# Seven quarter products in place of eight in the gate and up products of one feed-forward, with its hidden tiles in two passes

## The chip, the cores and the metric

One core of one Trainium2 chip runs the whole program. The metric is the device time of one execution, in microseconds (us). TensorE (PE in the profile) multiplies, with its weight loads shown apart as PEld; VectorE (DVE), ScalarE (ACT) and GpSimd (POOL) do the elementwise work; SyncE (SP) issues the weight transfers.

## The reference, cut to what matters

Two layers (DEPTH = 2) work on 256 latent and 256 context tokens of width 1024. Each layer has a feed-forward, a token-mixing part with three branches, and a second feed-forward. All arrays are float32.

```python
D_MODEL, SEQ, CTX_LEN, DEPTH, FFN_HIDDEN = 1024, 256, 256, 2, 2816

def swiglu(h, w_gu, w_down):
    g, u = jnp.split(h @ w_gu, 2, axis=-1)
    return (jax.nn.silu(g) * u) @ w_down

def ada_ffn_half(h, shift, scale, gate, norm_w, w_gu, w_down):
    return h + 0.5 * gate * swiglu(modulate(rms_norm(h, norm_w), shift, scale), w_gu, w_down)
```

The change is in the second layer's first `ada_ffn_half`. There `h` holds context and latent tokens together (512 columns), since the context is still read by the token mixing behind it. The second layer's second feed-forward works on the 256 latent tokens alone.

## The kernel before, in words

Activations lie feature by feature: 128 features in the partitions, tokens in the free dimension. `u` (the normed and modulated input) is 8 chunks of 128 features by 512 tokens. Weights come from HBM as a stream of panels of 128 x 2048 float32 (1 MB) in the order of use, into a ring of three (`RING`). A panel goes to the ring when the one three places before it has been left (`panel_left`, L899).

A float32 product is made of three matmuls on values rounded to a 32-bit format that TensorE reads faster (`fp32r`): hi x hi, lo x hi and hi x lo. For that, each half panel (128 x 1024, `HALF`) is rounded by ScalarE into `w_hi` (`round_half`, L972), and VectorE writes the rest, source minus rounded, into `w_lo` (`rest_of_half`, L2132). There are three places for halves (`HALVES`), so a half is rounded once the half three before it has been used (`half_used`). `split_matmul` (L1519) issues the three matmuls of one 128-deep step. Activations are split the same way: `u_hi`/`u_lo`, `hidden_hi`/`hidden_lo`.

A feed-forward (`ffn`) makes 22 hidden tiles (`FC`) of 128 features. A tile takes a gate product and an up product, each of 8 steps of three matmuls over all tokens (`std`), each in one PSUM bank; banks 0 to 3 are used in turn (`number[key] % 4`, `free_bank`). Tiles go in pairs: two gates, two ups. ScalarE takes the gate out of its bank with Silu (L1032), VectorE multiplies with the up bank (L2267), ScalarE rounds into `hidden_hi` (L1025), VectorE writes `hidden_lo` (L2273). When all 22 tiles are there, 8 down products (22 steps each) are made, and VectorE adds each, times the gate of the modulation, to `h` (`residual`, L2232).

Ahead of the feed-forward stands the norm (`norm`), in two parts of 256 tokens. VectorE scales a chunk into one of four slots of `sq` (L2172), ScalarE adds the shift and rounds into `u_hi` (L1004), VectorE writes `u_lo` (L2180); TensorE runs the first two gate tiles chunk by chunk behind it (`normed`, `streamed`).

Each engine's work is in program order, written by hand: the class `Splits` says between which other steps ScalarE and VectorE round the next halves. GpSimd has work only in the attention and delta parts (L920, L939, L949, L957); during the feed-forwards it has none.

In the last layer's later stages the 256-token activations are placed 48 elements further (`NARROW`), against weights that start at multiples of 64 elements.

Of the kernel before, what the change touches and what calls it, by code (L numbers as in the profile page):

```python
# [31 lines left out]
P = 128  # L32
# [37 lines left out]


# [68 lines left out]
def stream(inp):  # L140
# [150 lines left out]

def panel_kinds():
# [45 lines left out]


KINDS, START, ADA_AT = panel_kinds()  # L340
SPLITS = [n for n, k in enumerate(KINDS) if k == "split"]
N_PANELS = len(KINDS)


def product_owners():
# [52 lines left out]
    return number, owner, counts  # L398


def backbone(nc, wts, par_d, cst_d, mod_d, x_d, c_d, out_d):
    number, owner, counts = product_owners()

    split_before = np.cumsum([0] + [k == "split" for k in KINDS]).tolist()
    with ExitStack() as ctx:
# [3 lines left out]
        def sem(name):  # L409
# [41 lines left out]
        y_whole = [at("ya", 36, 4), at("yb", 40, 4), at("yc", 44, 4)]  # L451
        m_whole_hi = at("m_hi", 0, DC, F32R)
# [131 lines left out]

        def heads(ap):
# [24 lines left out]
        ab_read = sem("ab_read")  # L610
# [24 lines left out]
        gmv_root_ready = sem("gmv_root_ready")  # L635
# [37 lines left out]
        outs_rooted = sem("outs_rooted")  # L673
        outs_inverted = sem("outs_inverted")
# [3 lines left out]
        softplus_log = sem("softplus_log")  # L678
        decays_ready = sem("decays_ready")
# [3 lines left out]
        gamma_summed = sem("gamma_summed")  # L683
        gamma_read = sem("gamma_read")
# [2056 lines left out]
```

## Time and profile before

| | |
|---|---|
| median of 3 runs | 2488.67 us (2485.3 to 2489.74) |
| profiled execution, its own time | 2488.27 us |
| its span | 2486.5 us |
| PE busy | 2388.7 us (96%) |
| DVE busy | 1451.9 us (58%) |
| ACT busy | 942.5 us (38%) |
| POOL busy | 133.3 us (5%) |
| HBM read | 306 MB, 124 GB/s over the span |
| share of PE in the chain that ended last | 90% |

The profile gives times from the span's start. "PEclk" is the clock granted to TensorE, 1.00 being 2.4 GHz and 0.50 being 1.2 GHz. Matmul ends are modelled, so the spacing of starts tells more than the length of one. The gate and up products that the change touches begin at about 1462 us; those behind the first two gate tiles run from 1479.8 us.

### The profile page before, as it was taken

Reading aid. Unit: us, or ns where it says so; the run is one execution under the profiler, and the core shown is the slowest. Engines: PE = TensorE matmul, PEld = TensorE weight load, DVE = VectorE, ACT = ScalarE, POOL = GpSimd, SP = SyncE. Lnnn points to the kernel's source line nnn. Section 1 sums busy time; section 2 is a strip of 40 time slices with the busy share of each in tenths; the row PEclk is TensorE's granted clock in tenths of the full one; section 3 lists DMA queues with packets and bytes.
Section 4 is the critical chain, followed back from the end, with each engine's and each line's share of the span. In section 5 each row is a group of like instructions: output and inputs, shape, how many; then the busy total and the mean of one; then the engine's idle time right before and its main releaser. Section 6 shows DMA issues by size and latency. Waiting matters only on the chain.

```text
span 2486.5 us, 37740 instructions
## 1 busy us (share of the span) xinstructions
PE 2388.7 (96%) x15782; PEld 2028.2 (82%) x15782; DVE 1451.9 (58%) x2257; ACT 942.5 (38%) x1537; POOL 133.3 (5%) x170
## 2 busy tenths in 40 slices
PE   5999999999989999999999999999999988999999
PEld 4888888857878888888888888888886778899999
DVE  5877666356567465587755553333454657566655
ACT  2322223356544422233232232232244654444543
POOL 0000000003033000000000000000000203200000
PEclk8999999999999999999999999999999999999999
DMA  7545443211200043335554432222322220044554
GB/s 279 216 174 201 170 156 114 102 35 69 74 30 2 35 169 113 130 127 197 195 187 170 161 115 89 102 102 96 108 102 85 85 85 2 19 170 171 182 190 170
DMA packets 44664, 309.66 MB, mean 125 GB/s; under 512 B 5072, under 2 KB 6224, under 8 KB 7632
## 3 DMA queue, kind: packets, MB, share of 16 engines
q1 hardware_dynamic: 44208, 305.98, 33.8%
q8 instruction: 126, 2.06, 0.3%
q10 hardware_dynamic: 288, 1.27, 0.1%
q14 instruction: 42, 0.34, 0.0%
HBM read 306.18 MB, written 1.05 MB: 124 GB/s over the span
## 4 chain that ended last, share of the span: by engine, by line
PE 90%; DVE 5%; ACT 3%; issue 2%; DMA 1%; SPq 0%; POOL 0%; ACTq 0%; DVEq 0%
PE bank L1519 75%; PE bank L1876 7%; PE bank L1512 2%; PE bank L1793 1%; PE bank L1816 1%; DVE u_lo L2180 1%; DVE w_lo L2132 1%; PE bank L1802 1%; DVE sq L2172 1%; PE bank L1550 1%; ACT w_hi L972 1%; PE bank L1734 1%; DMA mod_par<-in_mod 0%; PE bank L1562 0%; ACT work L1290 0%
## 5 line engine op out<-in xcount | busy, mean ns | idle before, releaser
L2132 DVE TENSOR_TENSOR w_lo<-ring,w_hi 128x1024 fp32r<-128x1024 f32 x420 | 510.4, 1223 | 670.5 <-ACT w_hi L972 666.0
L1519 PE MATMUL bank<-u_hi,w_hi 128*128 128x512 f32 (+1 forms) x2272 | 813.8, 358 | 26.8 <-DVE w_lo L2132 13.9
L1519 PE MATMUL bank<-u_hi,w_lo 128*128 128x512 f32 (+1 forms) x2272 | 803.0, 353 | 0.0
L1519 PE MATMUL bank<-u_lo,w_hi 128*128 128x512 f32 (+1 forms) x2272 | 802.7, 353 | 0.0
L972 ACT ACTIVATE w_hi<-ring 128x1024 fp32r<-128x1024 f32 x420 | 443.0, 1059 | 818.8 <-PE bank L1519 804.5
L1519 PEld LDWEIGHTS bank<-u_hi,w_hi 128*128 128x128 f32 x2272 | 430.9, 190 | 95.6 <-issue 22.0
L1519 PEld LDWEIGHTS bank<-u_lo,w_hi 128*128 128x128 f32 x2272 | 431.0, 190 | 59.8
L1519 PEld LDWEIGHTS bank<-u_hi,w_lo 128*128 128x128 f32 x2272 | 431.0, 190 | 57.7
L1519 PE MATMUL bank<-hidden_hi,w_hi 128*128 128x512 f32 (+1 forms) x722 | 257.9, 357 | 0.0
L1519 PE MATMUL bank<-hidden_hi,w_lo 128*128 128x512 f32 (+1 forms) x722 | 257.2, 356 | 0.0
L1519 PE MATMUL bank<-hidden_lo,w_hi 128*128 128x512 f32 (+1 forms) x722 | 257.2, 356 | 0.0
L1876 PE MATMUL bank<-work 64*64 64x64 f32 (+1 forms) x3472 | 193.6, 237 | 30.9 <-DVE work L2617 11.3
L1876 PEld LDWEIGHTS bank<-work 64*64 64x64 f32 (+1 forms) x3472 | 174.1, 149 | 47.0 <-issue 17.2
L1519 PEld LDWEIGHTS bank<-hidden_hi,w_hi 128*128 128x128 f32 x722 | 135.6, 188 | 21.4 <-issue 1.6
L1519 PEld LDWEIGHTS bank<-hidden_lo,w_hi 128*128 128x128 f32 x722 | 135.7, 188 | 20.0
L1519 PEld LDWEIGHTS bank<-hidden_hi,w_lo 128*128 128x128 f32 x722 | 135.7, 188 | 19.9
L920 POOL TENSOR_TENSOR work<-work,small 128x512 f32<-128x512 f32 (+1 forms) x48 | 42.8, 897 | 1696.7 <-DVE small L2481 1696.4
L2113 DVE SCALAR_TENSOR_TENSOR ada_sum<-ring,cond,ada_sum 128x1024 f32<-128x1024 f32 x98 | 125.4, 1279 | 0.6
L1025 ACT ACTIVATE hidden_hi<-sg 128x512 fp32r<-128x512 f32 (+1 forms) x88 | 49.9, 579 | 146.6 <-DVE sg L2267 146.6
L2267 DVE TENSOR_TENSOR sg<-sg,bank 128x512 f32<-128x512 f32 (+1 forms) x88 | 53.1, 616 | 64.2 <-PE bank L1519 64.2
L1032 ACT ACTIVATE sg<-bank 128x512 f32<-128x512 f32 (+1 forms) x88 | 46.7, 535 | 114.8 <-PE bank L1519 114.8
L2113 DVE SCALAR_TENSOR_TENSOR rt<-ring,cond,rt 128x1024 f32<-128x1024 f32 x70 | 89.4, 1278 | 0.0
(234 smaller groups left out, 2451.4 us busy)
## 6 DMA issues: line engine op xcount, KB each, us to landing
ring<-in_wts SPq DMA_DIRECT2D x288, 1024.0 KB, 4.8
h<-in_x SPq DMA_DIRECT2D x8, 256.0 KB, 4.4
par<-in_par ACTq DMA_DIRECT2D x2, 620.0 KB, 5.9
out<-h SPq DMA_DIRECT2D x8, 128.0 KB, 3.5
cst<-in_cst SPq DMA_DIRECT2D x1, 704.0 KB, 12.2
mod_par<-in_mod SPq DMA_DIRECT2D x1, 96.0 KB, 12.1
cond<-in_c SPq DMA_DIRECT2D x1, 8.0 KB, 1.8
```

Source lines behind the costliest of these rows:

```text
L920: pool.tensor_tensor(some, some, ri[:, a % 4:a % 4 + 1].to_broadcast([P, keys.stop]), ALU.mult).then_inc(att_scaled, 1)
L972: act.activation(w_hi[:, b % HALVES, :], half_source(n % RING, part), ACT.Copy).then_inc(weights_rounded, 1)
L1025: act.activation(h_hi[:, 2 * i + c, 0:w], sg[:, c, 0:w], ACT.Copy).then_inc(hidden_rounded, 1)
L1032: act.activation(sg[:, c, 0:w], bank[(q0 + c) % 4][:, 0:w], ACT.Silu).then_inc(drained["a"], 1)
L1512: last = weights.used(pe.matmul(out, lhsT, rhs, start=n == 0, stop=n == len(parts) - 1))
L1519: last = weights.used(pe.matmul(out, lhs[a], rhs[b], start=start and n == 0, stop=stop and n == 2))
L1550: last = pe.matmul(bank[7 - unit % 2][32 * j:32 * j + 32, 0:256], C("pick")[:, 32 * s:32 * s + 32], total[:, j, :], start=s == 0, stop=s = ...
L1734: last = pe.transpose(bank[4 + n % 2][0:QK, hd * P:(hd + 1) * P], tile[:, at:at + QK], ident)
L1876: return pe.matmul(out, lhsT, rhs, start=start, stop=stop)
L2113: last = stt(total, panel[:, kk, :, :], cond[:, k, s:s + 1], total, ALU.mult, ALU.add)
L2132: tt(w_lo[:, b % HALVES, :], half_source(n % RING, part), w_hi[:, b % HALVES, :].bitcast(F32), ALU.subtract).then_inc(panel_left[n % RING] ...
L2267: tt(sg[:, c, 0:w], sg[:, c, 0:w], bank[(q0 + 2 + c) % 4][:, 0:w], ALU.mult).then_inc(drained["v"], 1)
```

## The change

For hidden tiles 2 to 21 (`PLAIN = 2` stay as they were) of layer 1's first feed-forward, gate and up are computed together by Strassen's scheme in Winograd's form. The panel of a tile is cut into four quarters (128 x 512, four steps of 128): "11" and "12" the gate weights for features 0 to 511 and 512 to 1023, "21" and "22" the up weights for the same. The activations are cut into features 0 to 511 and 512 to 1023, tokens 0 to 255 (EARLY) and 256 to 511 (LATE). Of these come:

- four sums of weight quarters for each tile, s1 = 21 + 22, s2 = s1 - 11, s3 = 11 - 21, s4 = 12 - s2, made by GpSimd into the four slots of `sq`;
- four sums of the activations ("folds"), made once by GpSimd from `whole`, the unrounded `u`, and split in hi and lo by ScalarE and VectorE;
- seven products a tile, each 4 steps of three matmuls over 256 columns, in half a bank each, in the order p1, p6, p2, p5, p7, p3, p4;
- four additions by VectorE that put gate and up together from them, into `sum_work`, one operand from PSUM and one from SBUF in each, and one copy of p1 by ScalarE.

A tile now has seven quarter units to round and rest, in place of two halves. `w_hi`/`w_lo` are flat, with six places for quarters, which are put 16 elements further (`SHIFT`). The hidden tiles go in two passes, 0 to 11 and 12 to 21, each followed by its own 8 down products (12 steps, then 10) and additions to `h`, since `whole`, the folds and `sum_work` take arena space of the hidden tiles. Semaphores of other stages are merged to free numbers; they order the same steps.

```diff
+SUMMED = ((1, 0),)
+PASSES = ((0, 12), (12, FC))
+PLAIN = 2
+SHIFT = 16
+SUM_PRODUCTS = (("p1", "a"), ("p6", None), ("p2", "v"), ("p5", None), ("p7", "v"), ("p3", None), ("p4", "v"))
+QUARTERS = ("11", "s2", "12", "s1", "s3", "s4", "22")
```

GpSimd:

```diff
+            def sums_of(l, f):
+                tt = pool.tensor_tensor
+                for i in range(PLAIN, FC):
+                    n = START[l, "sum", f, i]
+                    before = 6 * (sum_before[n] - 1)
+                    a11, a12, a21, a22 = [quarter_of(n, at) for at in range(4)]
+                    s1, s2, s3, s4 = [sq[:, at, :] for at in range(4)]
+                    pool.wait_ge(panel_in[n % RING], 16 * (n // RING + 1))
+                    if i == PLAIN:
+                        pool.wait_ge(tokens_summed, PART_AT[l, 2 * f] + len(PARTS[l, 2 * f]))
+                        pool.wait_ge(tokens_spread, PART_AT[l, 2 * f] + len(PARTS[l, 2 * f]))
+                    if before >= 0:
+                        pool.wait_ge(quarter_rest_ready, before + 4)
+                    tt(s1, a21, a22, ALU.add).then_inc(sums_made, 1)
+                    pool.wait_ge(sums_made, sum_count(n, "s1"))
+                    tt(s2, s1, a11, ALU.subtract).then_inc(sums_made, 1)
+                    if before >= 0:
+                        pool.wait_ge(quarter_rest_ready, before + 5)
+                    tt(s3, a11, a21, ALU.subtract).then_inc(sums_made, 1)
+                    if before >= 0:
+                        pool.wait_ge(quarter_rest_ready, before + 6)
+                    pool.wait_ge(sums_made, sum_count(n, "s2"))
+                    tt(s4, a12, s2, ALU.subtract).then_inc(sums_made, 1)
+                    if i == PLAIN:
...
+                        pool.wait_ge(whole_ready, 2 * DC * (SUMMED.index((l, f)) + 1))
+                        tt(t1, up[:, :, LATE], up[:, :, EARLY], ALU.subtract).then_inc(sums_made, 1)
...
```

ScalarE, ahead of the tiles:

```diff
+            def summed_ffn(l, f):
+                for part, places in enumerate(PARTS[l, 2 * f]):
+                    for k in range(DC):
+                        act.wait_ge(u_rest_ready, DC * (PART_AT[l, 2 * f] + part) + k + 1)
+                        for c, cols in places:
+                            act.activation(whole[:, k, cols], whole[:, k, cols], ACT.Identity,
+                                           bias=mods[:, l, 6 * f * DC + k, c:c + 1]).then_inc(whole_ready, 1)
...
+                plain_gate(0)
+                plain_gate(1)
+                splits.freed(first + 2)
...
```

TensorE, one tile:

```diff
+                def panel(i):
+                    for what, _ in SUM_PRODUCTS:
+                        key = (l, what, f, i)
+                        w2 = weights.quarter()
+                        free_bank(key)
+                        for k in range(4):
+                            last = split_matmul(bank_of(key)[:, LATE if what in ("p6", "p5", "p3") else EARLY],
+                                                [x[:, k, :] for x in w2], [x[:, k, :] for x in operands[what]], k == 0, k == 3)
+                        last.then_inc(product_made, 1)
...
```

VectorE, one tile:

```diff
+                def panel(i, at):
...
+                    splits.freed(u0)
+                    splits.freed(u0 + 1)
+                    if i > max(at, PLAIN):
+                        made(i - 1)
+                    splits.freed(u0 + 2)
+                    wait_product(dve, p2)
+                    wait_drained(dve, p1)
+                    tt(sum_work[:, c11:U2 + 1:U2 - c11, :], two(p2),
+                       sum_work[:, P1:P1 + 1, :].to_broadcast([P, 2, SEQ]), ALU.add).then_inc(drained["v"], 1)
+                    splits.freed(u0 + 3)
+                    if i > max(at, PLAIN):
+                        rest(i - 1, at)
+                    splits.freed(u0 + 4)
+                    wait_product(dve, p7)
+                    wait_drained(dve, p2)
+                    step(tt(sum_work[:, U3:U3 + 2, :], two(p7), sum_work[:, U2:U2 + 1, :].to_broadcast([P, 2, SEQ]), ALU.add))
+                    step.wait()
+                    tt(sum_work[:, c22, :], sum_work[:, U3, :], bank_of(p7)[:, LATE], ALU.add).then_inc(drained["v"], 1)
+                    splits.freed(u0 + 5)
+                    splits.freed(u0 + 6)
+                    wait_product(dve, p4)
+                    tt(sum_work[:, c21:c21 + 4:3, :], two(p4), sum_work[:, U3:U3 + 2, :], ALU.add).then_inc(drained["v"], 1)
+                    wait_drained(dve, p4)
```

(`splits.freed(v)` rounds or rests all units whose place is free once unit v - 1 has been used; `u0` is the tile's first unit.)

VectorE before, in the gate and up tiles: a round of this block serves two tiles (four halves, two products, two hidden rests).

```order
L2132 TENSOR_TENSOR w_lo<-ring,w_hi 128x1024 [waits weights_rounded] x4
L2267 TENSOR_TENSOR sg<-sg,bank 128x512 [waits drained_by_act,product_made] x2
L2273 TENSOR_TENSOR hidden_lo<-sg,hidden_hi 128x512 [waits hidden_rounded] x2
```

VectorE of the change, one tile (`panel`, from `splits.freed(u0)` to the addition of p4; L2482 is the rest of a unit, L2625 gate times up, L2630 the hidden rest, L2649, L2657, L2659 and L2663 the additions):

```order
L2482 TENSOR_TENSOR w_lo<-sq,w_hi 128x512 [waits weights_rounded,drained_by_dve]
L2482 TENSOR_TENSOR w_lo<-ring,w_hi 128x512 [waits weights_rounded]
L2625 TENSOR_TENSOR sum_work<-sum_work 128x512 [waits gated]
L2482 TENSOR_TENSOR w_lo<-ring,w_hi 128x512 [waits weights_rounded]
L2649 TENSOR_TENSOR sum_work<-bank,sum_work 128x2x256 [waits drained_by_act,product_made]
L2482 TENSOR_TENSOR w_lo<-sq,w_hi 128x512 [waits weights_rounded]
L2630 TENSOR_TENSOR some_lo<-sum_work,some_hi 128x512 [waits hidden_rounded]
L2482 TENSOR_TENSOR w_lo<-ring,w_hi 128x512 [waits weights_rounded]
L2657 TENSOR_TENSOR sum_work<-bank,sum_work 128x512 [waits drained_by_dve,product_made]
L2659 TENSOR_TENSOR sum_work<-sum_work,bank 128x256 [waits dve_step]
L2482 TENSOR_TENSOR w_lo<-sq,w_hi 128x512 [waits weights_rounded] x2
L2663 TENSOR_TENSOR sum_work<-bank,sum_work 128x2x256 [waits product_made]
```

Four instructions a tile on VectorE became thirteen. GpSimd, which had nothing here, has four a tile (the change; the first row waits for the rest of the tile before, whose s1 it overwrites):

```order
L1094 TENSOR_TENSOR sq<-ring 128x512 [waits quarter_rest_ready,panel_in0,sums_made]
L1096 TENSOR_TENSOR sq<-sq,ring 128x512 [waits sums_made]
L1099 TENSOR_TENSOR sq<-ring 128x512 [waits quarter_rest_ready]
L1103 TENSOR_TENSOR sq<-ring,sq 128x512 [waits sums_made,quarter_rest_ready]
```

ScalarE where the norm ends and the tiles begin, before:

```order
L1004 ACTIVATE u_hi<-sq,mods 128x256 [waits chunk_scaled] x3
L972 ACTIVATE w_hi<-ring 128x1024 [waits half_used]
L1032 ACT_TABLE_LOAD
L1032 ACTIVATE sg<-bank 128x512 [waits product_made] x2
```

and of the change:

```order
L1212 ACTIVATE u_hi<-whole,mods 128x256 [waits chunk_scaled] x3
L1231 ACTIVATE whole<-whole,mods 128x256 [waits u_rest_ready] x16
L1237 ACT_TABLE_LOAD
L1237 ACTIVATE plain_sg<-bank 128x512 [waits product_made] x2
L1180 ACTIVATE w_hi<-ring 128x1024 [waits half_used]
```

The half that the second up tile needs is now rounded behind sixteen additions of the shift, a table load and two Silus.

## Rows read from the trace of the kernel before

**Rows 1.** The page: busy time, share of the span and instructions of each engine.
```profile
PE 2388.7 (96%) x15782; PEld 2028.2 (82%) x15782; DVE 1451.9 (58%) x2257; ACT 942.5 (38%) x1537; POOL 133.3 (5%) x170
```

**Rows 2.** Stretch, length; PE, PEld, DVE, ACT, POOL busy (count); PEclk, DMA share, GB/s.
```profile
1482.00:1707.00 225.00, 225.00 (x994) 186.34 (x993) 78.78 (x84) 68.39 (x86) 0.00 (x0) 1.00 0.28 99
```

**Rows 3.** Timeline of PE, 512 columns: first and last of 55 rows.
```profile
1499.70 0.39 PE L1519 MATMUL bank<-u_hi,w_hi 128*128 128x512 f32 x1
...
1511.94 0.39 PE L1519 MATMUL bank<-u_hi,w_hi 128*128 128x512 f32 x1
```

**Rows 4.** The same, 256 columns, 48 elements further: first and last of 55.
```profile
2249.84 0.28 PE L1519 MATMUL bank<-u_hi,w_hi 128*128 128x256 f32 x1
...
2255.96 0.28 PE L1519 MATMUL bank<-u_hi,w_hi 128*128 128x256 f32 x1
```

**Rows 5.** The same, 256 columns, not moved: first and last of 20.
```profile
1472.00 0.28 PE L1519 MATMUL bank<-u_hi,w_lo 128*128 128x256 f32 x1
...
1474.28 0.28 PE L1519 MATMUL bank<-u_lo,w_hi 128*128 128x256 f32 x1
```

**Rows 6.** Groups by line and form, 1490 to 1600 us: busy, mean ns, idle before.
```profile
L2132 DVE TENSOR_TENSOR w_lo<-ring,w_hi 128x1024 fp32r<-128x1024 f32 x20 | 24.5, 1225 | 60.6 <-ACT w_hi L972 60.6
L2273 DVE TENSOR_TENSOR hidden_lo<-sg,hidden_hi 128x512 fp32r<-128x512 f32 x10 | 6.9, 689 | 0.5
L1025 ACT ACTIVATE hidden_hi<-sg 128x512 fp32r<-128x512 f32 x10 | 6.3, 632 | 20.1 <-DVE sg L2267 20.1
```

**Rows 7.** Timeline of DVE, end of the norm: start, us.
```profile
1471.01 0.48 DVE L2172 SCALAR_TENSOR_TENSOR sq<-h,scales,bank 128x256 f32<-128x256 f32 x1 [0.68 <-PE bank L1571]
1471.41 0.48 DVE L2180 SCALAR_TENSOR_TENSOR u_lo<-sq,mods,u_hi 128x256 fp32r<-128x256 f32 x1
...
1478.16 0.49 DVE L2180 SCALAR_TENSOR_TENSOR u_lo<-sq,mods,u_hi 128x256 fp32r<-128x256 f32 x1 [0.25 <-ACT u_hi L1004]
```

**Rows 8.** A group of POOL by form, whole span: busy, mean ns.
```profile
L920 POOL TENSOR_TENSOR work<-work,small 128x512 f32<-128x512 f32 x32 | 33.1, 1039 | 1688.4 <-DVE small L2481 1688.1
```

**Rows 9.** Timeline of POOL at 743 us, in the delta stage.
```profile
743.74 1.27 POOL L957 TENSOR_TENSOR rt<-work 128x512 f32<-128x512 f32 x1
...
744.97 1.73 POOL L957 TENSOR_TENSOR rt<-work 128x512 f32<-128x512 f32 x1
```

**Rows 10.** Timeline of DVE there.
```profile
744.65 0.91 DVE L2582 TENSOR_TENSOR work<-products_kept,work 128x512 f32<-128x512 f32 x1
...
745.48 1.76 DVE L2582 TENSOR_TENSOR work<-products_kept,work 128x512 f32<-128x512 f32 x1
```

**Rows 11.** Line L2582 in full: ns min/median/max by operand.
```profile
L2582 DVE TENSOR_TENSOR work<-bank,work x6: 652/662/674, 715.9 to 2117.3; 128x512 f32<-128x512 f32 x6
L2582 DVE TENSOR_TENSOR work<-products_kept,work x6: 906/1330/1762, 744.7 to 2148.6; 128x512 f32<-128x512 f32 x6
```

**Rows 12.** Timeline of ACT, norm to tiles.
```profile
1476.05 0.89 ACT L1004 ACTIVATE u_hi<-sq,mods 128x256 fp32r<-128x256 f32 x2
1477.55 0.51 ACT L1004 ACTIVATE u_hi<-sq,mods 128x256 fp32r<-128x256 f32 x1 [0.62 <-DVE sq L2172]
1480.61 1.06 ACT L972 ACTIVATE w_hi<-ring 128x1024 fp32r<-128x1024 f32 x1 [2.54 <-PE bank L1519]
1481.69 1.28 ACT L1032 ACT_TABLE_LOAD   x1
1482.98 1.09 ACT L1032 ACTIVATE sg<-bank 128x512 f32<-128x512 f32 x2
```

**Rows 13.** Busy time by stretch, ahead of the tiles; columns as in rows 2.
```profile
1458.00:1463.00 5.00, 3.14 (x24) 2.81 (x24) 3.88 (x8) 1.42 (x4) 0.00 (x0) 1.00 0.44 136
1463.00:1470.00 7.00, 7.00 (x33) 6.63 (x32) 4.25 (x13) 2.97 (x8) 0.00 (x0) 0.51 0.14 56
```

**Rows 14.** The same in the delta stage.
```profile
700.00:740.00 40.00, 31.91 (x598) 28.92 (x600) 26.00 (x63) 16.61 (x44) 17.39 (x22) 0.91 0.01 2
740.00:780.00 40.00, 37.47 (x656) 34.10 (x653) 29.87 (x76) 16.67 (x48) 17.03 (x20) 1.00 0.01 2
```

More of the change, by code:

```diff
@@ L186, in ffn @@
         a = ADA_FIRST
+        if (l, f) in SUMMED:
+            for what, n, i in summed_panels(l, f):
+                if what == "gu":
+                    std(gu, i * FFN)
+                elif what == "sum":
+                    chunk(gu, i * P)
+                    chunk(gu, FFN + i * P)
+                elif what == "ada":
+                    ada(carry, i)
+                elif i == 0:
+                    first, end = PASSES[n]
+                    blocks = down[first * P:end * P].reshape(end - first, P, DC, P).transpose(2, 0, 1, 3)
+                    for eight in blocks.reshape(end - first, 8, P, P):
+                        half(eight.transpose(1, 0, 2))
+            return
         for i in range(FC // 2):
@@ L289, with summed_panels @@
 MERGE_ADA = ((0, 0), (1, 0), (2, 0))
+def summed_panels(l, f):
+    out = [("gu", 0, 0), ("gu", 0, 1)]
+    for n, (first, end) in enumerate(PASSES):
+        out.extend([("sum", n, i) for i in range(max(first, PLAIN), end)])
+        out.extend([("down", n, i) for i in range((end - first) // 2)])
+    return out
 def panel_kinds():
@@ L305, in ffn @@
         start[l, "gu", f] = len(out)
+        if (l, f) in SUMMED:
+            for what, n, i in summed_panels(l, f):
+                if what == "ada":
+                    ada(carry, i)
+                    continue
+                if what == "sum":
+                    start[l, "sum", f, i] = len(out)
+                elif what == "down" and i == 0:
+                    start[l, DOWN[n], f] = len(out)
+                out.append("sum" if what == "sum" else "split")
+            return
         for i in range(FC):
@@ L583, in branches, with summed, scaled_chunk, sum_parts @@
             return [chunks_at(late(l), xs) for xs in (y_whole, y_whole_hi, y_whole_lo)]
+        def summed(l, i):
+            return i % 2 == 0 and (l, i // 2) in SUMMED
+        def scaled_chunk(l, i, k):
+            return whole[:, k, :] if summed(l, i) else sq[:, k % 4, :]
+        U2, U3, P1 = 8, 9, 11
+        def sum_parts(x):
+            first = 4 * x
+            return sum_work[:, first:first + 2, :], sum_work[:, first + 2:first + 4, :]
+        EARLY, LATE = slice(0, SEQ), slice(SEQ, T)
+        def folds(both):
+            return [both[n // 2][:, :, (EARLY, LATE)[n % 2]] for n in range(4)]
         def heads(ap):
@@ L1199, in _ @@
                 step.wait()
-                act.activation(t1, t1, ACT.Ln, bias=ones[:, 0:1]).then_inc(softplus_log, 1)
+                act.activation(t1, t1, ACT.Ln, bias=ones[:, 0:1]).then_inc(softplus_ready, 1)
                 def conv_in(c):
```

397 lines of the change are left out of this document (323 added, 74 removed).

## The prediction

> **What bounds the kernel now.** The page comes first: PE is busy for 96% of the span, no other engine for over 58% [rows 1]. The view by stretch then narrows this to the tiles that the change touches. From 1482 to 1707 us PE has no idle time at all and the full clock, DVE works 78.8 of 225 us, ACT 68.4, POOL nothing [rows 2]. Its pace is that of the column stream: 54 starts take 12.24 us, 0.2267 us for a matmul of 512 columns [rows 3]. A hidden tile (gate and up) has 48 of them, 10.88 us. So only fewer columns, or a stall, can change this stretch.
>
> **TensorE's part.** The change makes 84 matmuls of 256 columns of a tile. Where activations stand 48 elements past the weights' grid, 54 starts of 256 columns take 6.12 us, 0.1133 each [rows 4]; where both stand on it, 19 take 2.28 us, 0.12 each [rows 5]. The 16 elements by which the quarters are moved give the distance of rows 4 (0 less 16 is 48, counted by 64), so I take 0.1133: 9.52 us a tile, 1.36 a product. At 0.12 it is 10.08. Twenty tiles would win 20 x 1.36 = 27.2 us, if everything else kept pace.
>
> **VectorE's part.** A tile now takes thirteen instructions. One of 512 elements with both inputs in SBUF lasts 0.69 us [rows 6], with one input in PSUM 0.66 [rows 11]; neighbours overlap by some 0.09 (0.48 long, 0.40 apart [rows 7]), so I count 0.60 each. Seven unit rests, gate times up and the hidden rest: 9 x 0.60 = 5.4. The additions: p2 0.60; p7 0.73, since the next waits for its end; 256 columns 0.35; p4 0.73, with its wait. Together 7.8 of TensorE's 9.52 us. ACT has eight of 0.63 [rows 6] and two shorter, some 6 us, and is not the bound.
>
> **GpSimd's part decides.** It gets four sums of 128 x 512 a tile. The timeline in the delta stage shows what happens when GpSimd and a VectorE instruction with two SBUF inputs meet: the sum of L957 ends at 745.01 [rows 9], the VectorE product that began at 744.65 ends at 745.56 [rows 10], 0.55 later, though it needs 0.69 alone [rows 6]. GpSimd's next, begun at 744.97, ends at 746.70, 1.14 after that. VectorE's next ends at 747.25, again 0.55 later. They take turns: 1.14 us for one, 0.55 for the other, with about 0.14 of start hidden. With an input in PSUM the same line takes 0.66 beside GpSimd [rows 11], so the additions go on. Nine of thirteen instructions must take turns.
>
> Which price for a sum? L957 reads two streams and takes 1.27 alone, 1.14 behind a turn; L920, whose second input is one value repeated, takes 1.04 [rows 8], 0.90 behind a turn. The sums read two streams, so 1.14; the ends are 0.90 and 1.27.
>
> VectorE's round is then, by the order shown: s1 of the tile two ahead may start when VectorE has the rest of s1 of the next. From there: the rest of s3 0.55; sum s1 1.14 (beside it the p4 addition, hidden); rest of s4 0.55; s2 1.14; rest of 22 0.55; s3 1.14; gate times up 0.55; s4 1.14; rest of 11 0.55. That is 5 x 0.55 + 4 x 1.14 = 7.3. Then, with GpSimd done: p2, s2, hidden rest, 12 (4 x 0.60), p7 0.73, 0.35, s1 0.60: 4.1. **11.4 us a tile**, over the 10.88 of before. TensorE has five quarters in hand, which delays the moment but not the rate.
>
> The Trainium skill, "SBUF — State Buffer", section "SBUF: two separate sides", says that the pair of ports is an exclusive lock held for the whole instruction and that the other fully blocks. By that, nothing of the start would be hidden: 5 x 0.69 + 4 x 1.27 + 4.1 = 12.6 us a tile, an estimate from that page and rows 6 and 9, and the total would be some 19 us higher than mine. The turns in rows 9 and 10 show 0.55 and 1.14, so the shorter ones stand in the sum.
>
> **The sum**, against the profiled execution (2488.27 us, span 2486.5; 0.4 under the median of the runs):
> - Norm ahead of the tiles. The first four sums start when the second part's tokens are spread, 1471 us, while VectorE alternates a scaling (PSUM input) and a rest (two SBUF inputs) of 256 each, 0.79 a pair [rows 7], and TensorE follows it. A pair beside a sum takes 1.14 + 0.28 = 1.42. 4 x 0.63 = **+2.5**.
> - The second up tile. Its half of weights is rounded at 1480.61 and later in the ACT queue [rows 12]; now it stands behind 16 additions of 0.39 (1480.6 to 1486.8), the table load 1.28, two Silus 1.09: 1489.2, then 1.06 rounding [rows 12] and 1.23 rest [rows 6]: 1491.5. TensorE starts the first up tile at 1482.3 (1479.8 + 2.5) and is through at 1487.8. **+3.7.**
> - Clock. After 3.14 busy us of 5, the grant stood at 0.51 for the next 7 us [rows 13]. A stall of 3.7 behind a thin norm may bring one such stretch more: half speed for 6 us or so is **+3** (between 0 and 3.5).
> - First pass, ten tiles. Folds of 1024 elements on GpSimd (2.2 each at L957's rate) and their splitting hold VectorE's first round until some 13 us after the up tile. Then 8 x 11.4, then, with no sums in the last round, 1.2 to the last quarter's rest and 4.0 to the first half of the down weights: 109.4, against 108.8. **+0.6.**
> - Second pass, ten tiles. The first round runs at TensorE's 9.5 and 0.7 for its last addition, then 8 x 11.4, then 5.2: 106.6. **-2.2.**
> - The down products keep their 176 x 3 matmuls. Eight more additions to `h` lie beside 65 us of down products with VectorE mostly idle: 0. One panel fewer to load, DMA at a 0.28 share [rows 2]: 0. Renamed semaphores: 0.
>
> 2488.3 + 7.6 = **2496 us**, 0.3% slower. Sixteen rounds run at 11.4, so 0.1 us on the round counts 1.6 us.
>
> **The rivals.**
> - *Cheaper turns.* A plain sum costs L920's 0.90: 10.4 a round, 16 us less, **2480**. For it: L957 reads in four pieces of 128 columns. Against it: L920 streams one operand only. 14%.
> - *TensorE stays the bound.* The two engines hardly meet, or the engines' slack absorbs it: 9.52 a tile, 27.2 off, and the up tile's stall and the clock (6.7) on: **2468**; at 0.12 a matmul, 2479. Against it stand rows 9 to 11. 16%.
> - *The clock falls in the tiles (slower, much).* TensorE now stands still for 1.9 us of each 11.4, and the grant does fall with breaks: 0.91 in a stretch with PE busy 31.9 of 40 us, 1.00 at 37.5 [rows 14]. At half clock a tile takes 84 x 0.213 (256 columns at 1.2 GHz) = 17.9 us and binds; it decides from the point where over a fifth of the time is at half (9.52 + 8.4 x 0.22 = 11.4). If half is, 20 x (13.7 - 10.9) = +56, with the start 7 more, **2552**. For the forecast speaks that a 0.91 would leave TensorE at 10.5, still under 11.4. 8%. The Trainium skill, "TensorE: Matmul & The Clock Gate", section "A second HAM failure mode: psum-queue depth-cycling", describes this: frequent short breaks between groups of matmuls make the clock swing. Rows 14 bear it out for a stretch with PE 80% busy, only weakly.
> - The forecast keeps 62%.
>
> **How the numbers follow.** A measurement can tell about 0.2% from no change, 5 us: 2483.7 to 2493.6 is "same". The forecast's own range goes with 11.0 to 12.0 a round (-6, +10) and the start from 2 to 12: 2486 to 2509; of its 62%, some 44 lie above 2493.6, 14 inside, 4 below. The cheaper turns are below or inside (9 and 4), TensorE's bound below (16), the clock above (8). Faster 0.29, same 0.18, slower 0.53. The range reaches down to 2474, to take in the cheaper turns and the 0.12 variant, and up to 2512; 2468 and 2552 are left out.
>
> **What would show it.** In the changed profile: the view by stretch with PE busy about 85% in the tiles and DVE near 95%, POOL near 50%; the L2482 group of 512 elements with a mean well over 0.69 us (near 1.1); PE's idle time put down to `w_lo` L2482; 11.4 us from one tile's first p1 to the next; a break of 3 to 4 us ahead of the second up tile. Wrong if L2482 stays at 0.69 beside busy GpSimd, if PE has no idle time in the tiles, if GpSimd's sums last 1.04, or if the clock row shows fives there.

## The result and the profile after

The changed kernel takes 2506.1 us (median of 4 runs, 2502.4 to 2513.3) against 2489.2 for the kernel before: ratio 1.0069, 95% interval 1.0053 to 1.0086. It is slower. The forecast was 2496, with a range of 2474 to 2512 and 0.53 on slower: right in direction and range, but the loss is 16.9 us where the sum had 7.6. The profile is of the longest of the four executions (2513.3 us, span 2511.5).

The page of the changed kernel: busy time by engine and the granted clock (answers to [rows 1]).

```profile
PE 2383.2 (95%) x16508; PEld 2054.6 (82%) x16508; DVE 1613.2 (64%) x2455; ACT 992.2 (40%) x1675; POOL 273.4 (11%) x254
...
PEclk9999999999999999999999999999999999999999
```

The view by stretch: end of the norm, the up tiles, first pass, first down products, second pass; columns as in [rows 2].

```profile
1465.00:1482.00 17.00, 14.32 (x104) 12.72 (x102) 14.97 (x30) 9.58 (x21) 5.49 (x4) 1.00 0.04 17
1482.00:1501.00 19.00, 13.96 (x51) 10.98 (x51) 11.66 (x12) 14.73 (x26) 12.11 (x5) 0.82 0.16 56
1501.00:1616.00 115.00, 99.84 (x841) 97.89 (x841) 112.14 (x131) 50.42 (x96) 58.55 (x36) 0.99 0.26 92
1616.00:1681.00 65.00, 65.00 (x287) 53.80 (x288) 24.40 (x32) 15.02 (x17) 7.21 (x6) 1.00 0.28 98
1681.00:1790.00 109.00, 98.89 (x843) 97.43 (x842) 105.83 (x127) 50.65 (x95) 56.77 (x35) 1.00 0.27 97
```

In both passes VectorE is busy for 97% of the time, and TensorE, without idle time in [rows 2], for 87 and 91%. The bound has moved to VectorE. The clock stayed near full there although TensorE stops once a tile. It was at its half level from 1491.2 to 1498.1 us, in the up tiles (0.82 over their stretch), and from 1504.9 to 1508.3, at the head of the first pass (0.99 over that pass).

The timeline of VectorE for one tile: start, us, line, out<-in.

```profile
1528.91 0.68 DVE L2663 TENSOR_TENSOR sum_work<-bank,sum_work 128x512 f32<-128x512 f32 x1
1529.62 1.07 DVE L2482 TENSOR_TENSOR w_lo<-sq,w_hi 128x512 fp32r<-128x512 f32 x1
1530.81 1.59 DVE L2482 TENSOR_TENSOR w_lo<-ring,w_hi 128x512 fp32r<-128x512 f32 x1
1532.32 1.77 DVE L2625 TENSOR_TENSOR sum_work<-sum_work 128x512 f32<-128x512 f32 x1
1534.02 1.75 DVE L2482 TENSOR_TENSOR w_lo<-ring,w_hi 128x512 fp32r<-128x512 f32 x1
1535.69 0.68 DVE L2649 TENSOR_TENSOR sum_work<-bank,sum_work 128x512 f32<-128x512 f32 x1
1536.30 0.67 DVE L2482 TENSOR_TENSOR w_lo<-sq,w_hi 128x512 fp32r<-128x512 f32 x1
...
1541.07 1.07 DVE L2482 TENSOR_TENSOR w_lo<-sq,w_hi 128x512 fp32r<-128x512 f32 x1
```

And of GpSimd beside it.

```profile
1528.56 1.59 POOL L1094 TENSOR_TENSOR sq<-ring 128x512 f32<-128x512 f32 x1 [4.78 <-DVE w_lo L2482]
1530.23 1.62 POOL L1096 TENSOR_TENSOR sq<-sq,ring 128x512 f32<-128x512 f32 x1
1531.82 1.74 POOL L1099 TENSOR_TENSOR sq<-ring 128x512 f32<-128x512 f32 x1
1533.51 1.71 POOL L1103 TENSOR_TENSOR sq<-ring,sq 128x512 f32<-128x512 f32 x1
1540.00 1.59 POOL L1094 TENSOR_TENSOR sq<-ring 128x512 f32<-128x512 f32 x1 [4.78 <-DVE w_lo L2482]
```

The rest at 1529.62 comes again at 1541.07: a round of 11.45 us (11.4 was forecast). Four of VectorE's instructions with two SBUF inputs meet the four sums; their starts then lie 1.2, 1.5, 1.7 and 1.7 us apart instead of 0.60, so the four take 6.07 us (1529.62 to 1535.69) instead of 4 x 0.60 = 2.40. The addition with a PSUM input beside the first sum keeps its 0.68. GpSimd then waits 4.78 us for VectorE.

The waits from 1500 to 1600 us: us in total, times, longest.

```profile
POOL sq L1094 <- DVE w_lo L2482: 39.6, 9, 4.8
...
PE bank L1814 <- DVE w_lo L2482: 9.5, 6, 1.7
...
PE bank L1814 <- DVE fold_lo L2619: 2.3, 1, 2.3
```

The next table gives stages by the starts of TensorE's matmuls in the profiled executions: norm (first matmul of `u` to the first of 512 columns in the up tiles), up tiles, first ten summed tiles, last ten, and the time from tile to tile in the first pass (starts of VectorE's 256-column addition of p7). In the kernel before, ten tiles are 10 x 10.88. The runs shown below are in it too.

| kernel | median us | ratio to before, 95% | norm | up | pass 1 | pass 2 | a tile |
|---|---|---|---|---|---|---|---|
| before | 2489.2 | | 17.4 | 10.9 | 108.8 | 108.8 | 10.88 |
| changed | 2506.1 | 1.0053 to 1.0086 | 18.0 | 18.6 | 115.1 | 108.7 | 11.45 |
| tiny_sums | 2476.5 | 0.9934 to 0.9974 | 17.4 | 17.7 | 97.5 | 99.0 | 9.52 |
| rest_from_psum | 2477.3 | 0.9940 to 0.9971 | 18.0 | 18.6 | 96.5 | 99.0 | 9.42 |
| sums_on_vector | 2499.1 | 1.0015 to 1.0048 | 15.3 | 17.4 | 112.2 | 104.7 | 10.92 |
| half_ahead | 2509.5 | 1.0049 to 1.0110 | 20.0 | 11.4 | 122.4 | 108.7 | 11.45 |
| gate_later | 2489.1 | 0.9973 to 1.0003 | 17.5 | 16.5 | 107.9 | 100.0 | 10.33 |
| no_bubbles | 2479.6 | 0.9933 to 0.9970 | 17.5 | 11.0 | 108.4 | 99.0 | 9.95 |
| repeated_operand | 2486.7 | 0.9964 to 0.9992 | 17.0 | 18.9 | 105.8 | 100.5 | 10.45 |
| tiny_sums_no_shift | 2483.9 | 0.9955 to 0.9983 | 17.5 | 17.8 | 103.1 | 100.8 | 10.08 |
| folds_first | 2473.9 | 0.9914 to 0.9953 | 15.3 | 11.0 | 104.2 | 99.0 | 9.95 |

The norm holds a stretch at half clock in some profiles and not in others (changed, rest_from_psum, sums_on_vector, repeated_operand and folds_first: no; the other six: yes), so its column moves by some 2 us for that alone. The ratios are to the kernel before run beside each, whose medians were 2488.8 to 2490.8 us; between two changed kernels a difference of a few us is better read from the stage columns than from the medians.

### The profile page after: what moved, and what is told of

It is laid out like the page before. It is cut to its first block, busy times and chain, and to the rows that moved or that the text cites. A ratio compares the mean times of both kernels' runs of the same rounds, so it can differ in the third digit from the quotient of the medians.

```text
span 2511.5 us, 39867 instructions
## 1 busy us (share of the span) xinstructions
PE 2383.2 (95%) x16508; PEld 2054.6 (82%) x16508; DVE 1613.2 (64%) x2455; ACT 992.2 (40%) x1675; POOL 273.4 (11%) x254
## 4 chain that ended last, share of the span: by engine, by line
PE 80%; DVE 11%; ACT 4%; issue 3%; DMA 1%; SPq 0%; POOL 0%; ACTq 0%; DVEq 0%
PE bank L1814 66%; PE bank L2221 7%; DVE w_lo L2482 4%; PE bank L1807 2%; DVE sum_work L2625 1%; PE bank L2138 1%; ACT w_hi L1180 1%; PE bank L2161 1%; DVE u_lo L2528 1%; PE bank L2147 1%; PE bank L1845 1%; PE bank L2079 1%; DMA mod_par<-in_mod 0%; DVE sum_work L2657 0%; PE bank L1857 0%
## 5 line engine op out<-in xcount | busy, mean ns | idle before, releaser
L2482 DVE TENSOR_TENSOR w_lo<-ring,w_hi 128x1024 fp32r<-128x1024 f32 (+1 forms) x438 | 538.5, 1238 | 532.2 <-ACT w_hi L1180 526.0
L1814 PE MATMUL bank<-u_hi,w_hi 128*128 128x512 f32 (+1 forms) x2192 | 760.4, 347 | 53.1 <-DVE w_lo L2482 38.5
L1814 PE MATMUL bank<-u_hi,w_lo 128*128 128x512 f32 (+1 forms) x2192 | 747.9, 341 | 0.0
L1814 PE MATMUL bank<-u_lo,w_hi 128*128 128x512 f32 (+1 forms) x2192 | 747.6, 341 | 0.0
L1180 ACT ACTIVATE w_hi<-ring 128x1024 fp32r<-128x1024 f32 (+1 forms) x438 | 435.2, 998 | 729.6 <-PE bank L1814 717.0
L2221 PE MATMUL bank<-work 64*64 64x64 f32 (+1 forms) x3472 | 193.6, 237 | 31.0 <-DVE work L3053 11.4
L1814 PE MATMUL bank<-hidden_hi,w_hi 128*128 128x512 f32 (+1 forms) x540 | 189.1, 350 | 0.0
L1814 PE MATMUL bank<-hidden_hi,w_lo 128*128 128x512 f32 (+1 forms) x540 | 188.5, 349 | 0.0
L1814 PE MATMUL bank<-hidden_lo,w_hi 128*128 128x512 f32 (+1 forms) x540 | 188.5, 349 | 0.0
L1143 POOL TENSOR_TENSOR work<-work,cst 128x256 f32<-128x256 f32 x80 | 61.7, 791 | 309.7 <-DVE work L3045 274.6
L1814 PE MATMUL bank<-fold_hi,w_hi 128*128 128x256 f32 x320 | 89.3, 279 | 2.3 <-DVE fold_lo L2619 2.3
```

The source lines that it names most:

```text
L1143: pool.tensor_tensor(level[:, d, n % 2, :, :], mt[:, d, :, :], mask, ALU.mult).then_inc(level_ready[d], 1)
L1180: act.activation(rounded_at(u)[0], source(u), ACT.Copy).then_inc(weights_rounded, 1)
L1814: last = weights.used(pe.matmul(out, lhs[a], rhs[b], start=start and n == 0, stop=stop and n == 2))
L2221: return pe.matmul(out, lhsT, rhs, start=start, stop=stop)
L2482: tt(lo, source(u), hi.bitcast(F32), ALU.subtract).then_inc(ready, 1)
```

## Experiments

**GpSimd's load taken away.** Theory T: VectorE and GpSimd take turns at SBUF. Rival L: a chain of latencies sets the round.

```diff
-tt(s1, a21, a22, ALU.add)
+tt(s1[:, 0:4], a21[:, 0:4], a22[:, 0:4], ALU.add)      # s2, s3, s4 likewise
```

> GpSimd's four sums of a tile are made on 4 of 512 columns, so their work is nearly gone (most of s1 to s4 is left out). Theory T (turns: VectorE and GpSimd slow each other on SBUF): the rests of quarters fall from a mean of 1.36 us in L2482 to 0.69, VectorE needs 7.8 us a tile, and TensorE binds at 9.52 to 10.1 us a tile instead of 11.45. Sixteen rounds win 22 to 31 us and the norm wins 2.7: 2506 less 25 to 34 is 2472 to 2481 us. Rival L (a chain of latencies: quarter rounded, rest, matmul, place free again; GpSimd's load only happens beside it): the round stays at 11.2 to 11.5 us, 2500 to 2506.

Measured: 2476.5 us, 29.5 under the changed kernel. The groups by form from 1500 to 1600 us:

```profile
L2482 DVE TENSOR_TENSOR w_lo<-sq,w_hi 128x512 fp32r<-128x512 f32 x38 | 25.9, 689 | 3.7 <-ACT w_hi L1180 2.6
L2482 DVE TENSOR_TENSOR w_lo<-ring,w_hi 128x512 fp32r<-128x512 f32 x28 | 19.3, 691 | 6.6 <-ACT w_hi L1180 5.2
```

The same two groups of the changed kernel:

```profile
L2482 DVE TENSOR_TENSOR w_lo<-ring,w_hi 128x512 fp32r<-128x512 f32 x25 | 33.9, 1360 | 0.9
...
L2482 DVE TENSOR_TENSOR w_lo<-sq,w_hi 128x512 fp32r<-128x512 f32 x34 | 25.6, 773 | 0.3
```

From 1360 and 773 ns both fall to 690, TensorE binds at 9.52 us a tile in the first pass (9.89 in the second), and the whole loss with 13 us more is gone. All semaphores and their order were still there, so they alone don't set the round. But the sums were also ready sooner, and L could live on that; the next run decides. One part of the expectation missed: the norm did not win 2.7 in this profile (17.4 against 18.0), since its stretch at half clock is in it.

**GpSimd's load kept, the second SBUF input taken away.** Here the second input of each quarter's rest comes from a PSUM bank.

```diff
-tt(lo, source(u), hi.bitcast(F32), ALU.subtract)
+tt(lo, source(u), bank[6][:, :] if KINDS[n] == "sum" else hi.bitcast(F32), ALU.subtract)
```

> The rests of quarters take their second operand from a PSUM bank in place of w_hi (the lower half of those weights is then wrong); GpSimd keeps its four full sums. Theory T: only a VectorE instruction with two SBUF inputs takes turns with GpSimd. So the rests go to 0.66 to 0.70 us, the sums towards their 1.27 alone (1.3 to 1.45, since gate times up and the hidden rest still meet them), TensorE binds at 9.5 to 10.1 a tile, 2473 to 2483 us. Rival S (any reading of SBUF beside GpSimd is slow, one input or two): the rests stay over 1.0, the round stays over 10.9, over 2497. Rival L: 11.2 to 11.5 a tile, 2500 to 2506.

Measured: 2477.3 us, 9.42 us a tile by VectorE's additions. TensorE had no idle time from 1510 to 1590 us and kept its 0.1133 a matmul, 9.52 a tile; VectorE, late from the head of the pass, was catching up. Groups by form, 1500 to 1600 us:

```profile
L2483 DVE TENSOR_TENSOR w_lo<-sq,bank 128x512 fp32r<-128x512 f32 x38 | 25.2, 684 | 0.5
L2483 DVE TENSOR_TENSOR w_lo<-ring,bank 128x512 fp32r<-128x512 f32 x28 | 19.0, 681 | 4.5 <-ACT w_hi L1180 4.5
L2626 DVE TENSOR_TENSOR sum_work<-sum_work 128x512 f32<-128x512 f32 x10 | 14.4, 1436 | 0.8 <-ACT sum_work L1250 0.8
...
L1099 POOL TENSOR_TENSOR sq<-ring 128x512 f32<-128x512 f32 x9 | 11.7, 1300 | 6.0 <-DVE w_lo L2483 6.0
L1094 POOL TENSOR_TENSOR sq<-ring 128x512 f32<-128x512 f32 x8 | 10.4, 1299 | 29.2 <-DVE w_lo L2483 29.2
```

All four sums are made. Two of them now take their 1.30 us alone, the other two a mean of 1.40 and 1.71. Of VectorE's instructions beside them, only the one that still has both inputs in SBUF, gate times up (L2626), is slow, 1436 ns; the hidden rest (L2631), which has both there too, comes when GpSimd stands still, and keeps its 685. So the meeting costs something only to VectorE instructions with two SBUF inputs. Rivals S and L fall (the chain of waits is the same, the sums still last 1.30 to 1.71 us each, and from 1510 us on TensorE doesn't wait), and T is shown from both sides.

**What a turn costs GpSimd.**

```diff
-tt(s1, a21, a22, ALU.add)
+tt(s1, a21, a22[:, 0:1].to_broadcast([P, QUARTER]), ALU.add)      # s2, s3, s4 likewise
```

> The changed kernel, GpSimd's four sums still 512 columns long but with one column of the second input repeated (the sums of weights are then wrong). Theory P (a GpSimd instruction that reads two streams costs 1.14 behind a turn, one that reads a single stream 0.90): four sums x 0.24 less, the round 10.5 instead of 11.45, 16 x 0.95 = 15 less than the changed kernel's 2506: 2488 to 2494. Rival Q (GpSimd's price is set by the output and the turns, not by the second stream): the round stays at 11.3 to 11.45 and the time at 2503 to 2507.

Measured: 2486.7 us and 10.45 us a tile. The time is 1.3 us under the expected range, the round 0.05 under the expected 10.5. GpSimd's price behind a turn does hang on its second stream, as the prediction assumed in choosing 1.14 over 0.90: the rival of the cheaper turns was right about the price of such an instruction, but the sums of the change are not such.

**The pace of TensorE.**

```diff
-SHIFT = 16
+SHIFT = 0          # in tiny_sums
```

> As tiny_sums (GpSimd's sums on 4 columns), and the quarters are not moved by 16 elements (SHIFT 0 in place of 16). TensorE binds in both. Theory G (the distance between weights and activations, counted by 64 elements, sets the pace of matmuls of 256 columns): 0.12 us a matmul, 10.08 a tile in both passes against 9.52 and 9.89 measured in tiny_sums: 10 x 0.56 + 10 x 0.19 = 7.5 more than 2476.5, 2482 to 2486. Rival N (the pace does not hang on it, it changes by itself from stretch to stretch, as it did between tiny_sums' two passes): 2474 to 2479, with 9.52 or 9.89 a tile.

Measured: 2483.9 us, 7.4 over tiny_sums, 10.08 us a tile in both passes. The passes alone give the 7.4: 5.6 in the first, 1.8 in the second. In the first the shift of 16 elements is worth what rows 4 and 5 said, 84 x (0.12 - 0.1133) = 0.56 a tile; in the second, where the shifted matmuls ran at 0.1178, only 0.19.

**The stall ahead of the second up tile.** Moved in ScalarE's queue:

```diff
 for part, places in enumerate(PARTS[l, 2 * f]):
     for k in range(DC):
+        if n == 6:
+            splits.freed(first + 1)        # round the half here
+        n += 1
         act.wait_ge(u_rest_ready, ...)
```

> ScalarE rounds the second up tile's half of weights after 6 of the 16 additions to whole instead of behind all of them. Theory A (the stall ahead of the second up tile costs its 3.7 us and the clock stretch behind it): both go, 6 to 8 us less, 2498 to 2500. Theory B (the folds set the head of the first pass, since the first tile's p6 waits for them until 1504.7 whatever the up tile does): the folds start 1.1 us later, TensorE only waits at p6 for what it no longer waits at the up tile, and the gain is between -1 (a loss) and 3.5 (the clock stretch alone): 2502 to 2507. I hold B the likelier.

Measured: 2509.5 us, 2.5 over the range of theory B, and the changed kernel's time within the spread of both (2504.8 to 2514.0 against 2502.4 to 2513.3): nothing was gained. The up tiles fell from 18.6 to 11.4 us, and the first pass rose from 115.1 to 122.4. The timeline of TensorE in half_ahead shows where it went:

```profile
1494.04 0.28 PE L1817 MATMUL bank<-u_lo,w_hi 128*128 128x256 f32 x1
1503.92 0.55 PE L1817 MATMUL bank<-fold_hi,w_hi 128*128 128x256 f32 x1 [9.61 <-DVE fold_lo L2622]
```

and GpSimd's timeline in the changed kernel why:

```profile
1486.88 2.36 POOL L1108 TENSOR_TENSOR fold<-whole 128x1024 f32<-128x1024 f32 x1 [10.56 <-ACT whole L1231]
1489.33 2.35 POOL L1110 TENSOR_TENSOR fold<-whole,fold 128x1024 f32<-128x1024 f32 x1
1491.63 3.36 POOL L1111 TENSOR_TENSOR fold<-whole 128x1024 f32<-128x1024 f32 x1
1494.95 2.84 POOL L1113 TENSOR_TENSOR fold<-whole,fold 128x1024 f32<-128x1024 f32 x1
```

The folds begin when ScalarE has made the 16 additions and last 10.9 us; the first p6 needs them. TensorE only waited elsewhere. The stall and the head of the first pass are one loss, not two, and theory B stands.

**All of GpSimd's work on VectorE.** The obvious remedy, if turns cost more than the work.

```diff
-# GpSimd: sums_of(l, f), four sums a tile and four folds
+# VectorE, in rest_of_unit ahead of the rest of "11":
+tt(s1, a21, a22, ALU.add).then_inc(sums_made, 1)
+dve.wait_ge(sums_made, sum_count(n, "s1"))
+tt(s2, s1, a11, ALU.subtract).then_inc(sums_made, 1)
+tt(s3, a11, a21, ALU.subtract).then_inc(sums_made, 1)
+dve.wait_ge(sums_made, sum_count(n, "s2"))
+tt(s4, a12, s2, ALU.subtract).then_inc(sums_made, 1)
+# and t1 to t4 ahead of fold_rest
```

> GpSimd's sums and its four folds are made by VectorE instead; the result is the same. Theory T: VectorE has 7.8 + 4 x 0.60 + two waits of 0.13 = 10.3 to 10.5 us a tile with every instruction at its price alone, and binds at that. Against 11.45: sixteen rounds win 15 to 18, the norm 2.7 at most, and the folds take 4 x 1.15 on VectorE in place of 10.9 on GpSimd, worth 0 to 5 at the head of the first pass: 2482 to 2490 us. Rival L (latencies, not load): the sums stand in VectorE's own queue now, so the round grows by their 2.4 to over 11.5 and beyond, 2506 to 2530.

Measured: 2499.1 us, faster than the changed kernel but 9 over the expected range. Every instruction has its price alone (684 to 692 ns), yet the round is 10.92, not 10.4. The timeline of VectorE:

```profile
1543.67 0.68 DVE L2645 TENSOR_TENSOR sum_work<-bank,sum_work 128x512 f32<-128x512 f32 x1
1544.38 0.69 DVE L2464 TENSOR_TENSOR w_lo<-sq,w_hi 128x512 fp32r<-128x512 f32 x1
1545.57 0.69 DVE L2464 TENSOR_TENSOR w_lo<-ring,w_hi 128x512 fp32r<-128x512 f32 x1 [0.50 <-ACT w_hi L1143]
```

and of ScalarE:

```profile
1544.38 0.64 ACT L1213 ACTIVATE sum_work<-sum_work 128x512 f32<-128x512 f32 x1 [4.07 <-DVE sum_work L2645]
1544.92 0.61 ACT L1143 ACTIVATE w_hi<-ring 128x512 fp32r<-128x512 f32 x1
```

Half a microsecond a tile is idle time of the binding engine: ScalarE stood for 4.07 us at the tile's Silu, with a rounding behind it that VectorE needs next. In the changed kernel the turns hid most of this wait: the same group of rests (`ring`, 512 elements) has 0.9 us of idle time before it from 1500 to 1600 us, against 4.0 here.

**That rounding ahead of the Silu.** On top of sums_on_vector, in ScalarE's part of a tile.

```diff
 splits.freed(u0)
+splits.freed(u0 + 1)
 if i > max(at, PLAIN):
     gate(i - 1)
-splits.freed(u0 + 1)
```

> As sums_on_vector (all sums and folds on VectorE), and ScalarE rounds one more quarter ahead of the tile's Silu instead of behind it. In sums_on_vector VectorE's round was 10.92 us: 10.42 of work and 0.50 of idle time in front of one rest, put down to ScalarE's rounding, which stood in ScalarE's queue behind a Silu that waited 4.07 us for the p4 addition. If that is the reason, the idle time goes and the round is 10.42: 17 rounds x 0.50 = 8 to 9 us less than sums_on_vector's 2499.1, 2489 to 2493. Rival: the quarter's place is not free any earlier, or the Silu then comes late for gate times up: the round stays at 10.8 to 10.92 and the time at 2497 to 2501.

Measured: 2489.1 us, 10.33 us a tile. The idle time went, and with it the loss: no difference from the kernel before can be told.

**The gaps between dependent instructions, and the half ahead.** On top of gate_later.

```diff
 tt(s1, a21, a22, ALU.add).then_inc(sums_made, 1)
+tt(lo_of_11, ...).then_inc(quarter_rest_ready, 1)      # the rest of "11" between s1 and s2
 dve.wait_ge(sums_made, sum_count(n, "s1"))
...
 step(tt(sum_work[:, U3:U3 + 2, :], two(p7), ...))
+splits.freed(u0 + 5)
 step.wait()
 tt(sum_work[:, c22, :], ...).then_inc(drained["v"], 1)
-splits.freed(u0 + 5)
...
-wait_drained(dve, p4)                                   # now in made(i)
```

with half_ahead's edit on ScalarE.

> As gate_later, with the second up tile's half rounded after 6 additions (as in half_ahead), and on VectorE other instructions between each result and its reader: the rest of 11 between s1 and s2, one rest between the two additions of p7, the wait for p4's addition moved to its reader. Three gaps of 0.12, 0.12 and 0.11 us go: a round of 10.0 to 10.1 us, 17 x 0.35 = 6 less than gate_later. At the head of the first pass the folds are on VectorE (4.7 us for four, against 10.9 on GpSimd), so what half_ahead gave back at p6 should now be kept: 4 to 8 us. Together 2476 to 2483 us, under the kernel before (2489.7). Rival H (the head gives it back again): 2484 to 2487. Rival: another resource binds at over 10.4 a round, over 2486.

Measured: 2479.6 us, ratio 0.9951: faster than both kernels. VectorE now starts an instruction every 0.60 us without a break, 9.95 us a tile. Little of the 4 to 8 us expected at the head came, though the total lies in its range: the up tiles are 5.4 shorter than in gate_later (11.0 against 16.5), but the first pass is 0.5 longer, though nine shorter rounds alone give 9 x 0.38 = 3.4. So 3.9 of the 5.4 were given back at p6. VectorE's timeline shows an idle stretch behind the first sum:

```profile
1483.67 0.69 DVE L2445 TENSOR_TENSOR sq<-ring 128x512 f32<-128x512 f32 x1
1489.44 0.69 DVE L2448 TENSOR_TENSOR w_lo<-ring,w_hi 128x512 fp32r<-128x512 f32 x1 [5.08 <-ACT w_hi L1143]
```

**The folds first.** On top of no_bubbles.

```diff
 # VectorE, first summed tile only
-s1; rest of 11; s2; s3; s4; up(0); rests of s2, 12, s1; ...; t1; t2; t3; t4; their rests
+s1; s2; s3; s4; t1; t2; rest of 11; t3; rests of t1, t2; t4; up(0); rests of s2, 12, s1; ...; rests of t3, t4
 # ScalarE: rounds t1 and t2 right behind 11
```

> As no_bubbles, with the head of the first pass in another order. In no_bubbles TensorE stood still from 1493.1 to 1502.0 in front of the first p6, and VectorE had been idle for 5.08 us (1484.4 to 1489.4), since its next instruction, the rest of 11, waited for ScalarE, which made the 16 additions first. Now VectorE makes the other three sums and two folds ahead of that rest, and the folds and their splitting go ahead of the quarters. If that idle time on VectorE is what the head loses (VectorE binds the whole first pass), 4 to 6 us go: 2479.6 becomes 2474 to 2476. Rival: ScalarE (16 additions, table load, two Silus until 1488.9, then the folds) sets p6 anyway, or the order delays p1 or the quarters of the second tile: 0 to 2 us, 2478 to 2480.

Measured: 2473.9 us, ratio 0.9934, 15 us under the kernel before and 32 under the changed one. The view by stretch, columns as in [rows 2]:

```profile
1500.00:1600.00 100.00, 99.67 (x815) 97.15 (x814) 97.21 (x164) 53.32 (x95) 0.00 (x0) 1.00 0.32 115
1680.00:1780.00 100.00, 100.00 (x750) 95.72 (x750) 88.05 (x145) 49.07 (x80) 0.00 (x0) 1.00 0.34 116
```

The first p6 starts 3.0 us after p1's last matmul instead of 9.0, and the first pass takes 104.2 instead of 108.4. That is 4.2 of the 5.7 us between the two medians. TensorE is the bound again in the second pass (99.0 us, 0.1178 a matmul). Other orders of the folds, or one sum kept on GpSimd beside the PSUM additions, were not tried.

## Why the prediction was right, and where its sizes were off

- **TensorE's part** was right: 0.1133 us a matmul and 9.52 a tile where TensorE binds (tiny_sums), 0.12 without the shift. Not foreseen was a second pace of 0.1178 (9.89 a tile), below.
- **VectorE's part and the turns** were right. 7.8 of own work plus turns of 0.55 and 1.14 made 11.4; the round is 11.45. Not nine of VectorE's instructions take turns, as the prediction says at first, but four a round (its own sum has five, of which the rest of s3 runs just ahead of the first sum). The shares named ahead came too: VectorE busy for 97% (95 said), GpSimd 51 (50), TensorE 87 and 91 (85). The sums start 1.67, 1.59 and 1.69 us apart, the sum of the two turns (1.69). Each instruction looks longer than its turn (VectorE's up to 1.77, GpSimd's up to 1.74), because it is counted from its start and includes the other's turn; only the spacing shows the price. The Trainium skill, "SBUF — State Buffer", section "SBUF: two separate sides", has the pair of ports locked for a whole instruction, with the other fully blocked; that would make a pair 0.69 + 1.30 = 1.99 us by the lengths alone. The trace shows 1.67, so some 0.3 us of the two overlaps. Part of that is what neighbours on one engine overlap anyway: in rest_from_psum two of GpSimd's sums start 1.25 apart (1542.58, 1543.83) and VectorE's instructions 0.60, 1.85 together, so that some 0.2 is left for the meeting itself. That a VectorE instruction with two SBUF inputs is the one that blocks, as the same section says, agrees with rest_from_psum (684 ns against 1436).
- **The norm**: +2.5 forecast. In profiles without a half-clock stretch there it takes 18.0 us with the sums on GpSimd and 15.3 without (sums_on_vector): 2.7. Against the profile before, which has such a stretch [rows 13], only 0.6 shows.
- **The second up tile**: +3.7 for the stall and +3 for the clock, 6.7 together; the up tiles took 18.6 instead of 10.9, 7.8 more. TensorE waited 4.88 us there. The clock fell to its half level as forecast, during the wait; twelve matmuls then started 0.427 us apart instead of 0.2267, which is some 2.5 us. The 1.2 us too few in the stall are the meeting again: the half's rest started when the sum had it, but it was counted at its 1.23 us alone while GpSimd was making the folds. With the first quarter's rest behind it, the two took 5.36 us instead of some 1.8 (VectorE's timeline of the changed kernel):

```profile
1490.18 5.36 DVE L2482 TENSOR_TENSOR w_lo<-ring,w_hi 128x1024 fp32r<-128x1024 f32 x2 [7.27 <-ACT w_hi L1180]
```
- **The first pass** is the term that failed: +0.6 forecast, +6.2 measured. The head was counted as 13 us from the end of the up tile to VectorE's first steady round, where 17.3 passed (1500.8 to 1518.2). The sum names no cost for the meeting of the two engines there. The folds were taken at 2.2 us each, 8.8 together; they lasted 2.36, 2.35, 3.36 and 2.84, 10.9, since the later ones meet VectorE's rests, and they start only behind the 16 additions. Two of the folds' own four rests took 2.3 us beside the next tile's sums, the other two 1.2. half_ahead shows that the first p6 waits for these rests however early the up tiles end: with the stall ahead of it removed, the first pass took 7.4 us more. The remaining 1.3 us are 8 x 0.05 for the rounds and 6.1 instead of 5.2 behind them.
- **The second pass**: -2.2 forecast, -0.1 measured. Its first tiles, bound by TensorE, ran at 9.89 rather than 9.52, and the end took somewhat more.
- The down products, the loads and the additional additions to `h` cost nothing, as forecast.
- Added up against the profile before: 0.6 + 7.8 + 6.2 - 0.1 = 14.5. With the norm at like clocks (2.7) it is 16.6. That this lies beside the 16.9 between the medians is no proof: the two profiled spans differ by 25.0 us, of which 1.7 lie ahead of this feed-forward, 14.4 in it, 2.1 in the norm behind it, which ran partly at half clock, and 6.4 in the pace of the last feed-forward (below). Part of the forecast's hit is luck as well: the range was 38 us wide, and the head of the first pass alone was off by 4.3.
- **The rivals.** Cheaper turns: refuted by 11.45 against 10.45 with the repeated operand. TensorE stays the bound: refuted, but it is what happens once the meeting is gone (2476.5 and 2477.3 us, over the 2468 forecast for it, since the second pass ran at 0.1178). The clock falls in the tiles: refuted. TensorE stopped for up to 1.7 us once a tile, and the granted clock of the second pass was 1.00; the one half-clock stretch of the first (1504.9 to 1508.3) stands at its head, around the wait for the folds. The Trainium skill, "TensorE: Matmul & The Clock Gate", section "A second HAM failure mode: psum-queue depth-cycling", tells of a clock that swings with short breaks between groups of matmuls; here breaks of this size at 91% busy did not bring it about.

## What to carry to other kernels

Work given to an idle GpSimd is not free if VectorE's instructions meet it with two SBUF inputs: four sums that cost VectorE 0.60 us each (2.4 a tile) cost it 3.7 a tile when GpSimd made them. Count a meeting as the sum of both turns, and before moving work there, count what it takes on VectorE itself. Once an engine binds, look for its idle time in front of another engine's in-order queue (0.50 us a tile here) and for its gaps between dependent instructions (0.38). Price a meeting not only in the steady rounds but also at the head of a stage, where two rests of 1.8 us together took 5.36; and check there that a stall removed is not simply met again at the next wait.

## What the runs showed of the hardware that was not expected

The pace of 256-column matmuls is not fixed by addresses alone. The second layer's last feed-forward has the same matmuls in every kernel here, and ran at 0.1178 us a matmul in five of the eleven profiles and at 0.1133 in six. The changed kernel's profile, TensorE's timeline, first and last of 55 rows (54 intervals, 6.36 us):

```profile
2399.77 0.28 PE L1814 MATMUL bank<-u_lo,w_hi 128*128 128x256 f32 x1
...
2406.13 0.28 PE L1814 MATMUL bank<-u_lo,w_hi 128*128 128x256 f32 x1
```

half_ahead's, first and last of 57 rows (56 intervals, 6.35 us), which has the same instructions there:

```profile
2399.80 0.28 PE L1817 MATMUL bank<-u_lo,w_hi 128*128 128x256 f32 x1
...
2406.15 0.28 PE L1817 MATMUL bank<-u_hi,w_lo 128*128 128x256 f32 x1
```

The 1,584 matmuls of that stretch took 188.5 us in the first profile and 181.5 in the second. Each kernel was profiled once, so that one kernel has both paces is inferred: of the five profiled executions with the slower pace, four lay 4.4 to 7.3 us over their kernel's median and one 0.7 under it; the six with the faster pace lay 0.1 to 5.3 under theirs. The pace may thus be most of the spread between runs (2502.4 to 2513.3 for the changed kernel).

Within one execution the pace changes too. tiny_sums ran its first pass at 9.52 us a tile and its whole second at 9.89, and every second pass with the shift began at 0.1178. The changed kernel's went from there to 0.1133 at about 1720 us, when VectorE began to make it wait. In the summed tiles and the last feed-forward of all traces, no change between the two paces falls inside an unbroken row of starts: at each, two starts lie at least 0.15 us apart. But most breaks change nothing, and what decides is open. With the shift taken out, the pace was 0.12 in both passes.
